# Dilated attention: GpSimd lays q and k out by residue class, plain float32 values with a column of ones, V loaded for two heads together

## The reference, cut to what matters

```python
DIL_PATTERNS = ((128, 1), (512, 4), (2048, 16))    # (window, dilation)

def dilated_branch(q, k, v, dilation, radius):      # radius = window // (2 * dilation) = 64
    # tokens are split by residue: sequence r holds tokens r, r + dilation, r + 2 * dilation, ...
    # query a of a sequence sees the keys c of the same sequence with |c - a| <= radius
    s = einsum('bhrnqd,bhrnkd->bhrnqk', qb, kw) * (Dh ** -0.5)
    s = where(mask, s, NEG_INF)
    lse = logsumexp(s, axis=-1)
    o = einsum('bhrnqk,bhrnkd->bhrnqd', exp(s - lse[..., None]), vw)
    return o, lse

def dilated_attention(q, k, v):
    outs, lses = zip(*(dilated_branch(q, k, v, d, w // (2 * d)) for w, d in DIL_PATTERNS))
    w = softmax(stack(lses), axis=0)
    return sum(w[..., None] * stack(outs), axis=0)
```

## Time and profile before

| | |
|---|---|
| median of 3 runs | 3663.91 us (3659.92 to 3665.02) |
| profiled execution | 3657.93 us, its span 3656.1 us |
| PE busy | 3391.8 us, 93% |
| DVE busy | 1795.1 us, 49% |
| ACT busy | 1317.4 us, 36% |
| POOL busy | 630.6 us, 17% |
| mean granted TensorE clock | 0.972 |

### The profile page before, as it was taken

The page is one execution under the profiler, slowest core; times in us unless marked ns, Lnnn a source line. Parts: engine busy times, 40 slices in busy tenths (PEclk is TensorE's granted clock), DMA queues, the critical chain, the costliest instruction groups (busy, mean ns, idle before and its releaser), DMA issues. The chain is left out here.

```text
span 3656.1 us, 51666 instructions
## 1 busy us (share of the span) xinstructions
PE 3391.8 (93%) x18272; PEld 2919.9 (80%) x18272; DVE 1795.1 (49%) x3370; ACT 1317.4 (36%) x2718; POOL 630.6 (17%) x694
## 2 busy tenths in 40 slices
PE   8999995999999699993997999999999999997798
PEld 8988883888888699993776888888888888885677
DVE  5124344888888588883443333333343333333333
ACT  4111112777777577771222122121222112211332
POOL 2023330111111100001221222222222222221122
PEclk9999997999999899996998999999999999998899
DMA  5233336012300466744556111111231111112332
GB/s 184 98 107 125 118 107 167 19 46 56 77 19 19 104 145 163 174 116 141 184 173 208 57 46 46 46 46 52 83 124 46 47 56 46 46 46 113 104 108 90
DMA packets 279064, 342.75 MB, mean 94 GB/s; under 512 B 75248, under 2 KB 209264, under 8 KB 273648
## 3 DMA queue, kind: packets, MB, share of 16 engines
q1 hardware_dynamic: 278896, 340.59, 31.2%
HBM read 243.66 MB, written 96.86 MB: 93 GB/s over the span
## 5 line engine op out<-in xcount | busy, mean ns | idle before, releaser
L1553 DVE TENSOR_TENSOR e_h<-e_down_acc,e_h 128x512 f32<-128x512 f32 x512 | 350.4, 690 | 847.4 <-PE e_down_acc L89 847.4
L87 PE MATMUL e_up_acc<-e_xt_hi,e_up_hi 128*128 128x512 f32 x1024 | 399.3, 390 | 20.4 <-DVE e_xt_lo L1530 20.4
L88 PE MATMUL e_up_acc<-e_xt_lo,e_up_hi 128*128 128x512 f32 x1024 | 399.1, 390 | 0.0
L89 PE MATMUL e_up_acc<-e_xt_hi,e_up_lo 128*128 128x512 f32 x1024 | 399.0, 390 | 0.0
L87 PE MATMUL e_down_acc<-e_down_hi,e_u_hi 128*128 128x512 f32 x1024 | 398.3, 389 | 0.0
L88 PE MATMUL e_down_acc<-e_down_lo,e_u_hi 128*128 128x512 f32 x1024 | 398.3, 389 | 0.0
L89 PE MATMUL e_down_acc<-e_down_hi,e_u_lo 128*128 128x512 f32 x1024 | 398.3, 389 | 0.0
L630 DVE TENSOR_REDUCE c_neg_half<-c_scores 128x1 f32<-128x1024 f32 x256 | 313.1, 1223 | 84.7 <-PE c_scores L740 84.7
L1573 POOL TENSOR_TENSOR e_sq<-e_r 128x512 f32<-128x512 f32 x128 | 133.7, 1045 | 1006.8 <-ACT e_r L1509 1006.8
L583 ACT ACTIVATE c_e<-c_scores,c_neg_max 128x1024 f32<-128x1024 f32 x256 | 287.1, 1122 | 19.4 <-DVE c_neg_max L637 11.5
L758 PE MATMUL c_pv<-c_v,c_at 128*128 128x128 f32 x2048 | 270.1, 275 | 0.4 <-ACT c_o L597 0.4
(11 more groups left out here) (162 smaller groups left out, 7149.7 us busy)
## 6 DMA issues: line engine op xcount, KB each, us to landing
s_qkt<-a_hl SPq DMA_DIRECT2D x128, 256.0 KB, 2.8
e_up_raw<-w_up_dram SPq DMA_DIRECT2D x32, 1024.0 KB, 5.8
e_down_raw<-w_down_dram SPq DMA_DIRECT2D x32, 1024.0 KB, 4.9
b_kt<-s_qkt SPq DMA_DIRECT2D x64, 256.0 KB, 10.8
a_w_raw<-w_in_dram SPq DMA_DIRECT2D x24, 512.0 KB, 5.4
d_nd<-s_nd SPq DMA_DIRECT2D x48, 256.0 KB, 4.1
s_vg<-a_hl SPq DMA_DIRECT2D x32, 256.0 KB, 2.0
c_qs<-s_qkt SPq DMA_DIRECT2D x64, 128.0 KB, 2.8
```

The source lines that it names most:

```text
L87: nc.tensor.matmul(out, lhs_hi, rhs_hi, start=first, stop=False)
L88: nc.tensor.matmul(out, lhs_hi, rhs_lo, start=False, stop=False)
L89: return nc.tensor.matmul(out, lhs_lo, rhs_hi, start=False, stop=last)
L1553: nc.vector.tensor_tensor(h[:, slot(z, t), cols], down_acc[:, k % 4], h[:, slot(z, t), cols], ALU.add).then_inc(S["h"], 1)
```

## The change

Four things are altered together. V of the dilated heads is kept plain, without a hi and lo part: ACT's `v_hi` goes, DVE's `v_out` copies 256 columns, vg in DRAM is half as wide. In the dilated stage V is loaded for two heads at once into v, whose rows are 1 | V of the even head | V of the odd head | 1. A value matmul multiplies the plain float32 e by 65 columns, 64 of V and a column of ones whose product is the row sum; the exp no longer reads its accumulator, and POOL copies the sums out of nout (`sums`). POOL also copies q and k of each head into q4, k4, q16, k16, ordered by residue (`spread`), and the scores of patterns 1 and 2 read these with step 1. load_qk(h + 2) moves up behind the first store of a head and waits for the spreads of head h.

```diff
@@ projection: store_v, v_out
-                    if kind == 0:
-                        sp.dma_start(D["vd"][t * P:(t + 1) * P, pair * PW:(pair + 1) * PW], ...
-                    else:
-                        sp.dma_start(D["vg"][t * P:(t + 1) * P, pair * GROUP:(pair + 1) * GROUP], ...
+                    sp.wait_ge(v_done, j + 1)
+                    sp.dma_start(D[("vd", "vg")[kind]][t * P:(t + 1) * P, pair * PW:(pair + 1) * PW],
+                                 hl[:, j % 4, :PW].bitcast(F32)).then_inc(stored[j % 4], 16)
...
+                def v_out(n, t):
+                    j = n * TILES + t
+                    dve.wait_ge(acc_done, j + 1)
+                    if j >= 4:
+                        dve.wait_ge(stored[j % 4], 16 * (j // 4))
+                    nc.vector.tensor_copy(hl[:, j % 4, :PW].bitcast(F32), acc[:, j % BANKS, :PW]).then_inc(v_done, 1)
@@ dilated_phase, buffers
+        k4 = sb("k4", [P, 2, 4, SEQ // 4 + 2 * EDGE], F32R)
+        q4 = sb("q4", [P, 4, SEQ // 4], F32R)
+        k16 = sb("k16", [P, 2, 16, SEQ // 16], F32R)
+        q16 = sb("q16", [P, 16, SEQ // 16], F32R)
+        v = sb("v", [P, N_CHUNKS, VW])                  # VW = 2 * HD + 2, W1 = HD + 1
-        et_hi = sb("et_hi", [P, 2, 4, P], F32R)
-        et_lo = sb("et_lo", [P, 2, 4, P], F32R)
-        nout = sb("nout", [P, NP, TILES, HD])
+        et = sb("et", [P, 2, 4, P])
+        nout = sb("nout", [P, NP, TILES, W1])
@@ SP
                     if h >= 2:
-                        sp.wait_ge(S["scored"], (h - 1) * WORK)
+                        sp.wait_ge(S["scored"], (h - 2) * WORK + PAIRS)
+                        sp.wait_ge(S["spread4"], 3 * (h - 1))
+                        sp.wait_ge(S["spread16"], 3 * (h - 1))
...
-                        if h + 1 < HEADS:
+                        if h % 2 and h + 1 < HEADS:
                             sp.wait_ge(S["pv"], h * WORK + (p + 1) * PAIRS)
                             load_v(h + 1, p)
-                    if h + 2 < HEADS:
-                        load_qk(h + 2)
-                sp.wait_ge(S["exp"], 2 * TOTAL)
+                        if p == 0 and h + 2 < HEADS:
+                            load_qk(h + 2)
+                sp.wait_ge(S["md"], NP * HEADS)
@@ ACT, DVE
-                                             bias=neg_max[:, w % 4, s:s + 1],
-                                             accum_out=md_all[:, p, t, h, 1:2]).then_inc(S["exp"], 1)
+                                             bias=neg_max[:, w % 4, s:s + 1]).then_inc(S["exp"], 1)
-                    nc.scalar.copy(et_hi[:, w % 2, :c], turned[:, w % 2, :c]).then_inc(S["e_hi"], 1)
+                    nc.scalar.copy(et[:, w % 2, :c], turned[:, w % 2, :c]).then_inc(S["et"], 1)
-                    nc.vector.tensor_tensor(et_lo[:, w % 2, :c], turned[:, w % 2, :c], et_hi[:, w % 2, :c].bitcast(F32),
-                                            ALU.subtract).then_inc(S["e_lo"], 1)
-                    nc.vector.tensor_reduce(nout[:, p, t:t + 2], pv[:, w % 2, :, :2 * HD].rearrange(
-                        "p s (u d) -> p s d u", u=2), AX.X, ALU.add).then_inc(S["out"], 1)
+                        dve.wait_ge(S["md"], NP * (h - 1) + p + 1)
+                    nc.vector.tensor_copy(nout[:, p, t:t + 2],
+                                          pv[:, w % 2, :2 * W1].rearrange("p (s x) -> p s x", s=2)).then_inc(S["out"], 1)
@@ POOL
+                def spread(h, p):
+                    pool.wait_ge(q_in[h % 2], 64 * (h // 2 + 1))
+                    pool.wait_ge(k_in[h % 2], 128 * (h // 2 + 1))
+                    if h:
+                        pool.wait_ge(S["scored"], (h - 1) * WORK + (p + 1) * PAIRS)
+                    d, name = PATTERNS[p][1], (None, "spread4", "spread16")[p]
+                    q_out = (None, q4, q16)[p]
+                    by_class = lambda t: t.bitcast(F32).rearrange("p (k r) -> p r k", r=d)
+                    nc.gpsimd.tensor_copy(q_out[:], by_class(qs[:, h % 2])).then_inc(S[name], 1)
+                    for u in range(2):
+                        k_out = k4[:, u, :, EDGE:EDGE + SEQ // 4] if p == 1 else k16[:, u]
+                        nc.gpsimd.tensor_copy(k_out, by_class(kt[:, h % 2, u, EDGE:EDGE + SEQ])).then_inc(S[name], 1)
+
+                def sums(h, p):
+                    pool.wait_ge(S["out"], h * WORK + (p + 1) * PAIRS)
+                    nc.gpsimd.tensor_copy(md_all[:, p, :, h, 1], nout[:, p, :, h % 2 * HD]).then_inc(S["md"], 1)
...
+                spread(0, 1)
+                spread(0, 2)
+                for h in range(HEADS):
+                    for p in range(NP):
+                        sums(h, p)
+                        if p and h + 1 < HEADS:
+                            spread(h + 1, p)
@@ PE
+                    if w % WORK == PAIRS:
+                        pe.wait_ge(S["spread4"], 3 * (h + 1))
+                    if w % WORK == 2 * PAIRS:
+                        pe.wait_ge(S["spread16"], 3 * (h + 1))
...
-                        queries = qs[:, h % 2, first:first + (P - 1) * d + 1:d]
+                        queries = (qs[:, h % 2], q4[:, r % 4], q16[:, r])[p][:, first:first + P]
+                            if p == 0:
+                                keys = kt[:, h % 2, u, first:first + KEYS]
+                            elif p == 1:
+                                keys = k4[:, u, r, first:first + KEYS]
                             else:
-                                start = EDGE + first - RADIUS * d
-                                keys, dst = kt[:, h % 2, u, start:start + (KEYS - 1) * d + 1:d], out
+                                keys = k16[:, u, r - s:r - s + 2].rearrange("p r k -> p (r k)")
...
-                            nc.tensor.matmul(dst, et_hi[:, w % 2, s * chunks + c], v, start=(c == 0), stop=False)
-                            ins = nc.tensor.matmul(dst, et_lo[:, w % 2, s * chunks + c], v,
-                                                   start=False, stop=(c == chunks - 1))
+                            ins = nc.tensor.matmul(pv[:, w % 2, s * W1:(s + 1) * W1], et[:, w % 2, s * chunks + c],
+                                                   v[:, BASE[p] + r * CHUNKS[p] + j + c, side:side + W1],
+                                                   start=(c == 0), stop=(c == chunks - 1))
```

More of the change, by code:

```diff
@@ L783, in dilated_phase @@
     WORK = NP * PAIRS
-    EDGE = RADIUS * PATTERNS[1][1]
+    EDGE = RADIUS
+    VW = 2 * HD + 2
+    W1 = HD + 1
     KEYS = P + 2 * RADIUS
@@ L814, in dilated_phase @@
         md_stored = kit.sem("b_md_stored")
-        names = "scored masked negmax exp e_turn e_hi e_lo pv out"
+        names = "scored masked negmax exp e_turn et pv out spread4 spread16 md"
         S = {name: kit.sem("b_" + name) for name in names.split()}
@@ L879, in store @@
                         n = TILES // len(views)
-                        sp.dma_start(view, nout[:, p, r * n:(r + 1) * n]).then_inc(stored[p], 16)
+                        first = 1 - h % 2
+                        sp.dma_start(view, nout[:, p, r * n:(r + 1) * n, first:first + HD]).then_inc(stored[p], 16)
                 load_qk(0)
@@ L912, in exp, with e_copy @@
                         act.wait_ge(S["e_turn"], w - 3)
-                    h, p = head(w), pattern(w)
                     for s in range(2):
-                        t = w % PAIRS * 2 + s
                         nc.scalar.activation(used(w, e[:, w % 4])[:, s], used(w, masked[:, w % 4])[:, s], ACT.Exp,
-                                             bias=neg_max[:, w % 4, s:s + 1],
-                                             accum_out=md_all[:, p, t, h, 1:2]).then_inc(S["exp"], 1)
-                def e_hi(w):
+                                             bias=neg_max[:, w % 4, s:s + 1]).then_inc(S["exp"], 1)
+                def e_copy(w):
                     act.wait_ge(S["e_turn"], w + 1)
@@ L1000, in score @@
                         pe.wait_ge(k_in[h % 2], 128 * (h // 2 + 1))
+                    if w % WORK == PAIRS:
+                        pe.wait_ge(S["spread4"], 3 * (h + 1))
+                    if w % WORK == 2 * PAIRS:
+                        pe.wait_ge(S["spread16"], 3 * (h + 1))
                     if w >= 4:
                         pe.wait_ge(S["masked"], 2 * w - 6)
-                    d = PATTERNS[p][1]
                     for s in range(2):
                         r, j = tile_of(w, s)
-                        first = j * P * d + r
-                        queries = qs[:, h % 2, first:first + (P - 1) * d + 1:d]
-                        out = scores[:, w % 4, s]
+                        first = j * P
+                        queries = (qs[:, h % 2], q4[:, r % 4], q16[:, r])[p][:, first:first + P]
                         for u in range(2):
[L1010 to L1014, removed]
-                            else:
-                                start = EDGE + first - RADIUS * d
-                                keys, dst = kt[:, h % 2, u, start:start + (KEYS - 1) * d + 1:d], out
```

(18 more changed lines are left out.)

61 lines of the change are left out of this document (17 added, 44 removed).

## The result

The changed kernel takes 3690.5 us (3685.6 to 3695.4, 4 runs) against 3661.9 us of the kernel before beside it: ratio 1.0078, interval [1.0062, 1.0095]. Forecast were 3592 us, a gain of 72; measured is a loss of 0.8%. The predicted saving of PE's work is there and larger than predicted, and a stall that the prediction had set aside takes more than all of it.

The account below looks back on a forecast made before the run. PE was taken to bound the dilated stage. Scores and values save 9.1 us a head, 73 us over eight heads, less 1 and 0.5, giving 71.5 and a median of 3592 us; range 3582 to 3602.

Parts of the forecast that it names:

- the last of the rivals: Dilated stage: DVE and POOL hindering each other, held small, showing as longer POOL copies inside their range; no chance given.
- PE bounds the stage before: Dilated stage: PE, busy 47.8 of 48 us in one head, sets the time and stays the bound after.
- Scores from 1.11 and 1.03 to 0.56 us: Dense operands shorten first score to first value, saving 0.55 us an item in pattern 1 and 0.47 in pattern 2.
- Values not set by the moving columns: Weight loads pace value matmuls at 0.112 us a record, saving 0.05 us an item (patterns 0, 1), 0.02 (pattern 2).
- the 0.6 us a head for the changes of pattern: Dilated stage: time a head beyond its items, placed at pattern changes and kept in the 39.0 us forecast.
- the two rules: Value matmul pace: moving columns 0.057 us a record (fast rival, 3529 us, chance 0.17) or weight load 0.107 us (forecast).
- GpSimd's copy: Each POOL copy of 128x2048 in the dilated stage: 4.2 us taken, between 1.9 and 5.2; deadlines hold up to 5.3.
- GpSimd the bound, and slower than before: Rival: steps double POOL's copies, PE waits for spread4 and spread16; at 9.3 us a copy 3732 us; chance 0.08.
- The step costs POOL a factor of two: That rival's premise: steps of 4 and 16 elements make a POOL copy take twice 4.2 to 5.2 us.
- POOL's own loop: Argument against that rival: a POOL multiplication already needs 2 ns an element, so its loop, not reading, may set the pace.
- DMA, load_qk, V for two heads: Dilated stage loads: V at half the former bytes, 34 us of DMA work a head fits 38; hidden.
- Projection: Stage making V: less ACT and DVE work beside a PE busy 50.0 of 50 us; gain 0.

Follow-up runs that it names:

- the reduction: Changed kernel with the negation of the row maxima done by DVE's tensor_reduce (negate) instead of tensor_scalar; 3571.5 us, ratio 0.9758.
- 33 columns: Kernel with tensor_reduce as negation, its value matmuls over 33 columns instead of 65, half of V left out; 3570.3 us, one run.
- the product: Changed kernel with the negation as a tensor_tensor product of the maxima with a tile of -1, both inputs in SBUF; 3685.8 us.
- the kernel before with the copies: Kernel before the change with six POOL copies a head added that nobody reads; 3762.7 us, ratio 1.028.
- pieces of 1.1 us: Changed kernel with each POOL copy of 2048 columns cut into four of 512, negation still tensor_scalar; 3625.3 us, ratio 0.9927.

## Why the prediction was wrong

The failed step is the last of the rivals: "That DVE and POOL hinder each other I hold small". It looked at DVE's two big jobs, which read PSUM, and at a POOL row of a stage where hardly anything collides. It never listed DVE's small operations. It also looked for the sign on the wrong engine: POOL's copies are not longer than assumed, DVE's operation is. Before the change POOL was idle in this stage, so no wait of L951, the negation there, could be in the trace. But the projection of the same trace has something like it. A DVE operation with two inputs in SBUF runs twice for each step, once while POOL is in its second operation of 1.29 us and once with POOL idle:

```profile
229.40 2.54 POOL L385 TENSOR_TENSOR a_prod<-a_prod 128x512 f32<-128x512 f32 x2 [31.43 <-DVE a_prod L335]
231.40 1.10 DVE L342 SCALAR_TENSOR_TENSOR a_hl<-a_prod,a_hl 128x512 fp32r<-128x512 f32 x1 [0.88 <-ACT a_hl L272]
232.65 0.69 DVE L342 SCALAR_TENSOR_TENSOR a_hl<-a_prod,a_hl 128x512 fp32r<-128x512 f32 x1 [0.15 <-ACT a_hl L272]
```

All 32 that begin beside POOL take 1.07 or 1.10 us, the other 32 take 0.69. No run tests this pair, but it spoke against "small". The mistake was one of size too: a collision costs up to the length of what holds the other engine, 3.8 us, and not that of the 0.17 us operation that waits. Inside an item the negation stands on the chain scores, maximum, exp, turn, so 48 waits of 2.8 us more in the mean, 133 us in all, became 117 us of time, (1.0078 - 0.9758) x 3660. The lower clock is in these 117; its share wasn't measured alone.

The Trainium skill has this rule, in "SBUF — State Buffer", section "Who interferes with whom": VectorE and GpSimd share a pair of ports under an exclusive lock, held for a whole instruction, which VectorE wants in a two-port mode, or with two SBUF inputs while GpSimd reads SBUF. "VectorE: DVE Perf Modes" of the Trainium skill, section "What auto-detection actually checks", lets an operation with one source take the two-port mode where source and destination lie in SBUF and their outermost counts are even or equal; its table of modes has none above the plain one for tensor_reduce. The runs agree: tensor_scalar with two elements collides, a product of two SBUF tiles does, the reduction and the mask with one input in PSUM don't. That one element doesn't collide is what the run shows; these passages don't name that case. Seven waits of 5.1 to 14.1 us, in three runs, outlast the one instruction of which the page speaks; there the measurement decides. Applied to the negation, the rule would have told of a wait at each copy, and the prediction didn't draw on it.

Point by point:
- PE bounds the stage before: right; without the waits the time falls by about what PE sheds (8 x (48.0 - 36.8) = 90 us in its sequence, 85 measured).
- Scores from 1.11 and 1.03 to 0.56 us: right (1406.19 to 1406.75; 1413.87 to 1414.42).
- Values not set by the moving columns: right (33 columns change nothing). Mis-sized: records 0.104 us apart, not 0.112; items of 1.75, 1.75 and 1.09 us instead of 1.81, 1.83 and 1.16; and the 0.6 us a head for the changes of pattern don't appear (8 x 4.59 = 36.7, a head 36.8). So a head without waits lasts 36.8 us instead of 39.0, and the kernel with the reduction gains 85 us instead of 72. Of the two rules in "TensorE: Matmul & The Clock Gate" of the Trainium skill, that on weight loads fits, 0.107 against 0.104 measured. The section of the other, "Back-to-back issue gap", says itself that the formula counts too little for few columns, as it leaves out the weight loads; the prediction didn't say so.
- GpSimd's copy: 4.2 assumed, 3.8 measured; POOL is busy for 23 of 51 us a head, never late. PE never waited for spread4 or spread16. The rival "GpSimd the bound, and slower than before" had the direction right and the mechanism wrong: the kernel came out slower with POOL free for half the head.
- The step costs POOL a factor of two (1.90 to 3.90): what was held against it, POOL's own loop, was wrong; the copy without a step runs at the memset's pace. The prediction doubled a base of 4.2 to 5.2 us; the base is 1.90, so the doubled copy stayed below the 6.3 us from which POOL would set the pace.
- DMA, load_qk, V for two heads: hidden, as said; after the stage's start PE waits for no load. Projection: PE busy 225.1 of the first 240 us against 225.0 before, as said.

## What to carry to other kernels

Before giving an idle GpSimd a long copy, list every VectorE operation of the stage, the smallest too, and ask of each whether it has two SBUF inputs or takes one SBUF input to SBUF (here two elements a partition collided and one didn't). One such operation on the chain costs up to the length of the GpSimd instruction each time it meets one, 3 us for an operation of 0.17, and now and then the rest of GpSimd's unbroken row. A reduction, a single column or ScalarE did the same work without the wait. Check it by the maximum of a group's length, since its median shows nothing.

## What the runs showed of the hardware

- DVE and a back-to-back row of POOL instructions: in the changed kernel DVE got in at the first boundary each time (48 waits, 3.4 us at most). With the product, and in the kernel before with the copies, one wait of 13.7 us each ran past three copies; with pieces of 1.1 us five waits took 5.1 to 14.1. All seven ended 0.02 to 0.03 us after the last instruction of the row, none at a boundary in between. Cutting the work into pieces lowered the usual price and did not cap the rare one.
- A plain float32 matmul of 65 or of 33 columns stands in the trace as two weight loads and two matmul records, 0.104 us apart.
- A step of 4 or 16 elements doubles a POOL copy of 2048 elements, from 1.90 us to 3.6 to 4.0. In each of three traces (changed kernel, reduction, kernel before with copies) every copy with the step of 16 is shorter than every one with the step of 4, by 0.06 us or more (3.68 to 3.74 against 3.83 to 3.88 in the changed kernel). Why is open.
